# Gate/up weights of the middle pairs in 4 MB transfers of 32 KB rows, in a decoder block with a mixture of experts

## What is computed

```python
x = x + mix @ w_out[l]
x = x + moe_ffn(rms_norm(x, ffn_norm_w[l]), router_w[l], router_b[l], w_gate_up[l], b_gate_up[l], w_down[l], b_down[l])
return rms_norm(x, final_norm_w)
# moe_ffn, for the rows of one expert e:
gu = xb @ w_gate_up[e] + b_gate_up[e]          # 1024 -> 2048
gate, up = gu[:, :D_FF], gu[:, D_FF:]
gate = jnp.minimum(gate, SWIGLU_LIMIT)
up = jnp.clip(up, -SWIGLU_LIMIT, SWIGLU_LIMIT)
act = (up + 1.0) * (gate * jax.nn.sigmoid(SWIGLU_ALPHA * gate))
return (act @ w_down[e] + b_down[e]) * g[:, None]
```

## Time and profile before

| | |
|---|---|
| time, median of 3 runs | 1090.88 us (1090.13 to 1090.94) |
| profiled execution | 1090.8 us, span 1089.3 us |
| PE busy | 1030.9 us, 95% |
| DVE, ACT, POOL busy | 228.9, 119.6, 10.1 us |
| DMA | 423.69 MB, mean 389 GB/s |
| HBM read | 422.41 MB |
| chain that ended last | PE 65%, DMA 28%, DVE 5% |

### The profile page before, as it was taken

How to read it: one execution, slowest core, us unless ns; L and a number is a source line. 1 busy time by engine, 2 the same in 40 slices (tenths; PEclk the granted TensorE clock), 3 DMA queues, 4 the chain that set the end, 5 groups by cost and what they waited for, 6 DMA issues and landing times.

```text
span 1089.3 us, 12299 instructions
## 1 busy us (share of the span) xinstructions
PE 1030.9 (95%) x4971; PEld 443.2 (41%) x4971; DVE 228.9 (21%) x508; ACT 119.6 (11%) x287; POOL 10.1 (1%) x25
## 2 busy tenths in 40 slices
PE   7999998999999999989999999899899999999996
PEld 6686554343343332424242424233242434343422
DVE  3476444111111110111110111111011111111111
ACT  1133430000000000000000000000000000000001
POOL 0000000000000000000000000000000000000000
PEclk9999999999999998999999999999999999999999
DMA  9926545999999999999999999999999999999995
GB/s 307 396 107 243 196 182 211 427 429 428 430 427 430 427 430 427 429 428 430 427 430 428 428 428 428 428 429 428 430 428 428 428 428 428 430 427 430 427 428 210
DMA packets 35808, 423.69 MB, mean 389 GB/s; under 512 B 6016, under 2 KB 6032, under 8 KB 11120
## 3 DMA queue, kind: packets, MB, share of 16 engines
q1 hardware_dynamic: 33888, 422.80, 92.1%
q10 hardware_dynamic: 1904, 0.67, 0.2%
HBM read 422.41 MB, written 1.05 MB: 389 GB/s over the span
## 4 chain that ended last, share of the span: by engine, by line
PE 65%; DMA 28%; DVE 5%; ACT 1%; issue 1%; SPq 0%; DVEq 0%; POOLq 0%; POOL 0%; ACTq 0%
PE psum L819 25%; DMA dn_ring<-in_w_down_dram 21%; PE psum L834 18%; DMA gu_ring<-in_w_gate_up_dram 7%; PE psum L776 6%; PE psum L566 5%; PE psum L544 3%; PE psum L663 3%; PE psum L571 2%; DVE shared L1199 1%; DVE shared L1195 1%; DVE shared L1197 1%; PE psum L616 1%; DMA xres<-in_x_dram 0%; ACT shared L518 0%
## 5 line engine op out<-in xcount | busy, mean ns | idle before, releaser
L819 PE MATMUL psum<-gu_ring,shared 128*64 128x512 f32 x2048 | 446.8, 593 | 4.7 <-DMA gu_ring<-in_w_gate_up_dram 4.7
L834 PE MATMUL psum<-dn_ring,shared 128*64 128x512 f32 x1024 | 241.0, 622 | 32.4 <-DMA dn_ring<-in_w_down_dram 30.9
L819 PEld LDWEIGHTS psum<-gu_ring,shared 128*64 128x64 f32 x2048 | 144.2, 137 | 286.8 <-issue 274.4
L834 PEld LDWEIGHTS psum<-dn_ring,shared 128*64 128x64 f32 x1024 | 73.1, 142 | 181.9 <-issue 133.6
L1195 DVE TENSOR_SCALAR shared<-psum 128x512 f32<-128x512 f32 x32 | 22.1, 692 | 397.1 <-PE psum L819 397.1
L1138 DVE TENSOR_TENSOR shared<-posm,iota 128x256 f32<-128x256 f32 x47 | 20.0, 425 | 290.9 <-PE psum L544 290.5
L516 ACT ACTIVATE shared<-psum 128x512 f32<-128x512 f32 x32 | 19.1, 597 | 439.8 <-PE psum L819 439.8
L795 PE MATMUL psum<-shared 64*128 64x512 f32 x264 | 65.6, 615 | 0.7 <-ACT shared L509 0.7
L776 PE MATMUL psum<-shared,xres 128*128 128x128 f32 x512 | 63.0, 282 | 0.8 <-DVE shared L1108 0.8
L776 PEld LDWEIGHTS psum<-shared,xres 128*128 128x128 f32 x512 | 61.7, 197 | 1.7 <-DVE shared L1108 1.7
L566 PE MATMUL psum<-gu_ring 128*128 128x256 f32 x256 | 59.5, 391 | 0.2 <-ACT gu_ring L406 0.2
(11 more groups left out here) (142 smaller groups left out, 354.5 us busy)
## 6 DMA issues: line engine op xcount, KB each, us to landing
gu_ring<-in_w_gate_up_dram SPq DMA_DIRECT2D x128, 2048.0 KB, 26.4
dn_ring<-in_w_down_dram SPq DMA_DIRECT2D x64, 2048.0 KB, 23.4
gu_ring<-in_w_in_dram SPq DMA_DIRECT2D x11, 1024.0 KB, 16.4
dn_ring<-in_w_out_dram SPq DMA_DIRECT2D x4, 1024.0 KB, 8.7
gu_ring<-in_w_in_dram SPq DMA_DIRECT2D x2, 512.0 KB, 6.7
out_dram<-hmix SPq DMA_DIRECT2D x4, 256.0 KB, 2.0
dn_ring<-in_b_gate_up_dram SPq DMA_DIRECT2D x3, 256.0 KB, 15.7
xres<-in_x_dram ACTq DMA_DIRECT2D x1, 512.0 KB, 4.8
```

The source lines that it names most:

```text
L819: last = mm(bank[2 + b][CAP * c:CAP * (c + 1), :], xg[:, k, CAP * half:CAP * (half + 1)], gu_ring[:, 8 * half + k, w0:w0 + 512], start=Fal ...
L834: last = mm(bank[4][CAP * c:CAP * (c + 1), :], actT[:, a0:a0 + CAP], dn_ring[:, k // 2, w0:w0 + 512], start=False, stop=(k == KT - 1), ski ...
```

## The change

`gu_v` gets j = 4: a partition holds four rows that lie together, 32 KB. `load_gu_wide` loads two adjacent slots in one transfer of 4 MB, a packet of 32 KB per partition, on semaphores of its own (`gu_wide_in`). `load_gu` stays for 2 MB transfers; each of its packets is half of such a 32 KB row. Pairs 0 and 1 (`FIRST = 2`) and 13 to 15 (`LAST = 3`) are loaded narrow, pairs 2 to 12 wide: there SyncE waits for two quarters used before it issues one transfer, and TensorE waits once per two quarters. SyncE's written-out tail, with w_down moved ahead, begins one pair later. TensorE has pairs 0, 1, 13, 14 and 15 written out and a loop over the 11 between. The gather and `ffn_p` follow the new order of rows.

```diff
--- before.py
+++ after.py
@@ -44,7 +44,7 @@
 FAR = 1e30
 WS = 2048
 GUN, DNN = 8, 2
-LAST = 5
+FIRST, LAST = 2, 3
 
 
 def moe_block(nc, x, attn_norm_w, w_in, lq1, lk1, lq2, lk2, subln_w, w_out, ffn_norm_w, router_w, router_b,
@@ -141,6 +141,7 @@
         w_in_in = [sem(f"w_in_in{i}") for i in range(12)]
         w_out_in = [sem(f"w_out_in{i}") for i in range(4)]
         gu_in = [sem(f"gu_in{i}") for i in range(GUN)]
+        gu_wide_in = [sem(f"gu_wide_in{i}") for i in range(GUN // 2)]
         dn_in = [sem(f"dn_in{i}") for i in range(DNN)]
         fw_in = sem("fw_in")
         out_done = sem("out_done")
@@ -253,13 +254,18 @@
                     sp.dma_start(gu_ring[:, s, :].rearrange("p (k c) -> p k c", k=2),
                                  w_in_v[:, 2 * q:2 * q + 2, D * g:D * (g + 1)]).then_inc(w_in_in[s], 16)
             w_out_v = w_out.rearrange("o (k p) c -> p (o k) c", p=P)
-            gu_v = w_gate_up[0, :, :, :].rearrange("e (q p j) c -> p e q (j c)", p=P, j=2)
+            gu_v = w_gate_up[0, :, :, :].rearrange("e (q p j) c -> p e q (j c)", p=P, j=4)
             dn_v = w_down[0, :, :, :].rearrange("e (q p k) c -> p e q (k c)", p=P, k=4)
 
             def load_gu(e, half, q):
                 s = 4 * half + q
                 sp.dma_start(gu_ring[:, 2 * s:2 * s + 2, :].rearrange("p (e j) c -> p e (j c)", e=1),
-                             gu_v[:, bass.ds(e, 1), q, :]).then_inc(gu_in[s], 16)
+                             gu_v[:, bass.ds(e, 1), q // 2, 2 * WS * (q % 2):2 * WS * (q % 2 + 1)]).then_inc(gu_in[s], 16)
+
+            def load_gu_wide(e, half, h):
+                s = 2 * half + h
+                sp.dma_start(gu_ring[:, 4 * s:4 * s + 4, :].rearrange("p (e j) c -> p e (j c)", e=1),
+                             gu_v[:, bass.ds(e, 1), h, :]).then_inc(gu_wide_in[s], 16)
 
             def load_dn(e, q):
                 sp.dma_start(dn_ring[:, 2 * q:2 * q + 2, :].rearrange("p (e j) c -> p e (j c)", e=1),
@@ -303,17 +309,29 @@
                     sp.wait_ge(dn_used, j * (2 * DNN) + (q + 1))
                     load_dn(e, q)
 
-            with sp.Fori(0, more * PAIRS + (PAIRS - LAST)) as j:
+            def load_gu_half_wide(j, e, half):
+                for h in range(2):
+                    sp.wait_ge(gu_used, j * GUN + (4 * half + 2 * h + 2))
+                    load_gu_wide(e + half, half, h)
+
+            for i in range(FIRST - 1):
+                e = 2 * i + 2
+                load_gu_half(i, e, 0)
+                load_dn_second(i, e - 1)
+                load_gu_half(i, e, 1)
+                load_dn_first(i, e)
+            with sp.Fori(0, more * PAIRS + (PAIRS - FIRST - LAST)) as i:
+                j = i + (FIRST - 1)
                 e = ((j + 1) % PAIRS) * 2
-                load_gu_half(j, e, 0)
+                load_gu_half_wide(j, e, 0)
                 load_dn_second(j, (j % PAIRS) * 2 + 1)
-                load_gu_half(j, e, 1)
+                load_gu_half_wide(j, e, 1)
                 load_dn_first(j, e)
-            for i in range(PAIRS - LAST, PAIRS - 1):
+            for i in range(PAIRS - LAST - 1, PAIRS - 1):
                 j = more * PAIRS + i
                 e = 2 * i + 2
                 for half in range(2):
-                    before = max(0, 3 - (2 * (i - (PAIRS - LAST)) + half))
+                    before = max(0, 3 - (2 * (i - (PAIRS - LAST - 1)) + half))
                     load_gu_half(j, e, half, range(before))
                     if half == 0:
                         load_dn_second(j, e - 1)
@@ -474,8 +492,8 @@
                 if g == NH:
                     act.wait_ge(scores_read, NH)
                     act.dma_start(rw, router_w.rearrange("o (k p) e -> p (o k) e", p=P)).then_inc(rw_in, 16)
-                    act.dma_start(ffn_p[:, :].rearrange("p (q j) -> p q j", j=2),
-                                  ffn_norm_w.rearrange("o (q p j) -> p (o q) j", p=P, j=2)).then_inc(ffn_in, 16)
+                    act.dma_start(ffn_p[:, :].rearrange("p (q j) -> p q j", j=4),
+                                  ffn_norm_w.rearrange("o (q p j) -> p (o q) j", p=P, j=4)).then_inc(ffn_in, 16)
             keep_mixT(NH - 1)
 
             for a in range(TT):
@@ -772,7 +790,7 @@
                 for k in range(KT):
                     b, c = 2 + k // 4, P * (k % 4)
                     for a in range(TT):
-                        rows = xres[:, a, :].rearrange("t (q p j) -> t q j p", p=P, j=2)[:, k // 2, k % 2, :]
+                        rows = xres[:, a, :].rearrange("t (q p j) -> t q j p", p=P, j=4)[:, k // 4, k % 4, :]
                         last = mm(bank[b][:, c:c + P], rows, sel[:, a, :, :].rearrange("p e n -> p (e n)"),
                                   start=(a == 0), stop=(a == TT - 1))
                     if k % 4 == 3:
@@ -808,11 +826,13 @@
                     for c in range(2):
                         add_bias(2 + b, c, FF * b + 512 * c, half)
 
-            def gate_up(j, half):
+            def gate_up(half, narrow, wide):
                 for k in range(KT):
                     s = 4 * half + k // 2
-                    if k % 2 == 0:
-                        pe.wait_ge(gu_in[s], j * 16 + 16)
+                    if narrow and k % 2 == 0:
+                        pe.wait_ge(gu_in[s], 16 * narrow)
+                    elif not narrow and k % 4 == 0:
+                        pe.wait_ge(gu_wide_in[2 * half + k // 4], wide * 16 + 16)
                     for b in range(2):
                         for c in range(2):
                             w0 = FF * b + 512 * c
@@ -837,12 +857,12 @@
                     if k % 4 == 3:
                         last.then_inc(dn_used, 1)
 
-            def expert(j, half, last_one=False):
+            def expert(j, half, narrow=0, wide=0, last_one=False):
 
                 def nth(m, c):
                     return j * (2 * m) + (m * half + c)
 
-                gate_up(j, half)
+                gate_up(half, narrow, wide)
                 list(combine(nth(1, 1)))
                 for c in range(2):
                     last = add_bias(4, c, 2 * FF + 512 * c, half)
@@ -871,11 +891,16 @@
             pe.wait_ge(rounds_ready, 1)
             more = pe.value_load(more_rounds[0:1, 0:1], min_val=0, max_val=ROUNDS - 1)
             gate_up_bias(1, 0, 1)
-            with pe.Fori(0, more * PAIRS + (PAIRS - 1)) as j:
-                expert(j, 0)
-                expert(j, 1)
-            expert(more * PAIRS + (PAIRS - 1), 0)
-            expert(more * PAIRS + (PAIRS - 1), 1, last_one=True)
+            for j in range(FIRST):
+                expert(j, 0, narrow=j + 1)
+                expert(j, 1, narrow=j + 1)
+            with pe.Fori(0, more * PAIRS + (PAIRS - FIRST - LAST)) as i:
+                expert(i + FIRST, 0, wide=i)
+                expert(i + FIRST, 1, wide=i)
+            for i in range(LAST):
+                j = more * PAIRS + (PAIRS - LAST + i)
+                expert(j, 0, narrow=FIRST + 1 + i)
+                expert(j, 1, narrow=FIRST + 1 + i, last_one=(i == LAST - 1))
             for last in combine(more * (2 * PAIRS) + (2 * PAIRS + 1)):
                 last.then_inc(acc_done, 1)
```

## The result

The changed kernel takes 1103.97 us (median of 4 runs, 1102.44 to 1104.89) beside 1090.75 us for the kernel before in the same sessions: a ratio of 1.0119, 95% interval 1.0107 to 1.0131. The profiled execution has a span of 1101.8 us, 12.5 us more than before.

What follows compares the result with a forecast made beforehand. The prediction took the unbroken DMA weight stream (428 GB/s) as the bound, plus 25.0 us of serial work after the last gate/up landing. Packets -2.4 and code +0.5 gave -1.9: 1089.0 us, range 1086.8 to 1091.6.

Steps and rivals of the forecast that it cites:

- Gather and ffn_p: Gather's weights operand steps 16 B instead of 8 B: zero; three gathers in the tail 0.5 us either way.
- The margin of the tail: Last pairs, tail one pair shorter: 5.12 us less catching up from a margin of 5.6 us, 0.5 stays; price zero.
- TensorE never waiting in the last two pairs (margin used up): Sign that the forecast is wrong: TensorE has no waits near the end, the tail's margin being used up.
- The packets: Gate/up loads of pairs 2 to 12 in 32 KB packets: 352 fewer per engine, 2.4 us gained.
- The written-out code: TensorE's four more bodies, 8 to 9 more instruction packets on q8: 0.5 us lost.
- rival 2: Cost sits at the ends of transfers, 135 ns each, 44 fewer: 5.9 us gained, 1085.5 us; chance 0.14 with between.
- 18 packets on q8: Sign that the forecast is right: about 18 instruction packets on queue q8.
- the coarser waits: SyncE and TensorE wait per 4 MB transfer, 3.4 and 4.9 us later, hidden by queued work and landed slots: zero.
- the pitch: Rival 4: 32 KB pitch of narrow transfers lowers the rate, 4.3 us per 1%: 1093 to 1095 us; chance 0.06.
- rival 3: All new instruction packets fall on one DMA engine, at least 5.5 us lost: 1094.0 us; chance 0.06.

Runs made afterwards that it cites:

- gather_only: The kernel before with only the new order of rows (gather, `ffn_p`, `gu_v` with j = 4), all transfers 2 MB: 1103.82 us, ratio 1.0120.
- step3: The kernel before with a gather that reads columns at a step of 12 B (wrong columns): 1095.2 us, one run.
- narrow_code: The changed kernel's code, tail and semaphores, but 2 MB transfers of 16 KB rows, row order and gather as before: 1092.43 us, ratio 1.0012.
- big16: The changed kernel with 4 MB transfers in packets of 16 KB, order of rows and gather as before: 1092.11 us, ratio 1.0013.
- wide_step2: The changed kernel with the gather's line put back to 8 B step, its columns not matching the weight rows: 1088.80 us, ratio 0.9980.

## Why the prediction was wrong

**The step that failed** is "Gather and ffn_p": "Zero", with 5 ns per matmul, 0.5 us in all, as its bound. A gather took 3.68 us more (7.45 instead of 3.77). Its loads lasted 132 ns longer each (329 - 197); they overlap one another, so 115 ns of that reach the pace ((120.7 - 61.7) us for 512 loads), and 32 of them make the 3.7 us. I had read the price of a 16 B step from the chain's spans of two kinds of transposes, 0.76 us for four and 0.37 us for two. Those are spans of matmuls that overlap and wait for their operands. The loads of the same instructions, kept apart by form, said otherwise already in the kernel before; four of `act_t` at 16 B step, then two of the contiguous selection (busy us, mean ns | idle before):

```profile
L544 PEld LDWEIGHTS psum<-ident,shared 128*128 128x128 f32 x4 | 0.6, 209 | 0.4 <-DVE shared L1199 0.4
```

```profile
L544 PEld LDWEIGHTS psum<-ident,shared 128*128 128x128 f32 x2 | 0.2, 140 | 0.8 <-issue 0.8
```

A load at 16 B step was 69 ns longer there. In the gather 32 loads follow each other; its PEld group was busy 61.7 us of the 63.0 us of its matmuls, so the loads set its pace and time lost on them would be paid. These rows would have given the sign but not the size: 32 x 69 ns is an estimate of 2.2 us per gather, and a load of the gather turned out to pay about twice the 69 ns.

**The margin of the tail was right, and would have told.** The prediction had 5.6 us of margin in the last pairs, of which 0.5 stays once one more pair is held, and three gathers behind it. With 3.68 us for each they take 11.0 us, 10.5 more than the margin: its own sum would have come out slower. The rest of the 12.9 us is read from the chain. TensorE leaves the last place where both kernels are held 2.7 us later (836.28 against 833.60), as the stream itself starts late: between 150 and 200 us the DMA moved 243 GB/s instead of 273, which is 3.5 us of transfers, about one gather (in gather_only, without wide packets, it is 3.3 us, 836.89 against 833.60). The pair that is held once more takes 58.43 us and not 58.78. Together 10.5 + 2.7 - 0.3 = 12.9. The prediction named no rival in which TensorE becomes the bound, but among its signs of being wrong stands "TensorE never waiting in the last two pairs (margin used up)", and that is what came.

Room over the whole span is no measure of this. Never held, TensorE would have started the last quarter of gate/up in the kernel before at 253.71 + 14 x 53.66 + 10.4 = 1015.4, 48.9 us early, and at a step of 12 B the 16 gathers take only 1.8 us more each (5.54 instead of 3.77), 28 us in all. Yet in that run (step3) the last quarter starts 4.4 us later than in the kernel before:

```profile
1068.67 3.65 PE L819 MATMUL psum<-gu_ring,shared 128*64 128x512 f32 x16 [0.32 <-DMA gu_ring<-in_w_gate_up_dram]
```

w_down still stands seven times in its chain, from 454.89 to 807.10: what TensorE has in hand before that is spent on waits there. What counts is the start of the stream and the few pairs behind the last of these waits.

**The rest of the sum held by luck: two errors cancel.** Without the step the change gives 1088.8, where 1089.0 was forecast. The packets gained 3.6 us, not 2.4: by the estimate above a packet costs about 10 ns beside its bytes, more than the 5.6 to 7.5 worked out from the 4 KB packets; why is open. The written-out code cost 1.6 us (narrow_code), not 0.5. The reading of 135 ns per end of transfer (rival 2) is refuted by big16.

**Right:** 18 packets on q8 (8 more, as worked out); the coarser waits cost nothing (wide_step2 has them and no hole in its stream); without the dearer gather the margin of the tail sufficed (wide_step2), with the last quarter still waited for 1.2 us; no loss by the pitch; not all code on one engine (rival 3: narrow_code would be at 1096).

## What to carry to other kernels

A new layout for a transfer has a second reader: before pricing the transfer, ask at which byte step each engine will now read what it is matched with, and look up that operand's load by form, not the span of the matmuls around it. Then hold the extra time against the margin of the last pairs, not against the room over the whole span: here the DMA stays the slower one per pair (58.4 us against 57.35), and 3.7 us more per pair still set the end, so that the gain elsewhere is worth nothing. If a layout forces a wide step, copy once in the wanted order in a hole of another engine: here two copies of 2 us bought back 15.

## What the runs showed of the hardware

A weight load of 128x128 float32 takes 192 to 197 ns at steps of 4 and 8 B, 261 at 12 B, 329 at 16 B and 335 at 32 B; a copy of 128x1024 float32 on ScalarE takes 2.06 us with its input at 16 B step, where another pass (square) over contiguous input takes 1.05. A load of a transpose, 128x128 float32, takes 140 ns contiguous and 209 at 16 B step. A 32 KB packet instead of two of 16 KB saves about 10 ns on its engine (an estimate, 3.6 us for 352) at a rate already at 428 GB/s; 4 MB transfers instead of 2 MB in the same packets save nothing measurable (1092.11 against 1092.43 us). A pitch of 32 KB in HBM instead of 16 KB leaves the rate at 428 GB/s. Written-out TensorE code costs 0.15 to 0.3 us per instruction packet of 16 KB beside a full weight stream (1.4 us for 9, and 1.2 us for 4), while TensorE's wait for the last quarter stays the same (1.2 us); how is open.
